# Two latent heads of a pair scored on two row halves of TensorE, with one shared block of rotated keys

## What is computed

```python
def mla_q(zcq, g, w_uq, tabs):
    q = (rms_norm(zcq, g) @ w_uq).reshape(B, L, MLA_HEADS, MLA_NOPE + MLA_ROPE)
    q_nope, q_pe = jnp.split(q, [MLA_NOPE], axis=-1)
    if tabs is not None:
        q_pe = axial_rope(q_pe, tabs)
    return jnp.concatenate([q_nope, q_pe], axis=-1)
...
    k_pe = zkr.reshape(B, L, 1, MLA_ROPE)
    if tabs is not None:
        k_pe = axial_rope(k_pe, tabs)
    k = jnp.concatenate([k_nope, jnp.broadcast_to(k_pe, (B, L, MLA_HEADS, MLA_ROPE))], axis=-1)
...
o_m = block_attention(ql_m, [context keys, latent keys], values, MLA_SCALE)   # softmax(q k^T) v
```

## Time and profile before

| | us |
|---|---|
| Median of 3 runs (945.21 to 947.04) | 945.35 |
| Time of the profiled execution | 945.68 |
| Its span, first to last instruction | 943.8 |
| PE busy | 905.8 (96%) |
| DVE busy | 557.8 (59%) |
| POOL busy | 512.2 (54%) |
| ACT busy | 430.0 (46%) |

### The profile page before, as it was taken

How to read it: one execution, slowest core, us unless ns; L and a number is a source line. 1 busy time by engine, 2 the same in 40 slices (tenths; PEclk the granted TensorE clock), 3 DMA queues, 4 the chain that set the end, 5 groups by cost and what they waited for, 6 DMA issues and landing times.

```text
span 943.8 us, 13413 instructions
## 1 busy us (share of the span) xinstructions
PE 905.8 (96%) x4645; PEld 641.5 (68%) x4645; DVE 557.8 (59%) x903; ACT 430.0 (46%) x879; POOL 512.2 (54%) x433
## 2 busy tenths in 40 slices
PE   5999999999999999999999899999999999999996
PEld 4777767889744565665678789888894445555584
DVE  6669043513578679963218838667246758983337
ACT  6332121414566466655334862235335646655432
POOL 3346223324577755565547437454438886666672
PEclk9999999999999999999999999999999999999999
DMA  9968671214624200020353212223243221020252
GB/s 320 294 224 272 209 248 61 81 38 103 141 52 101 52 18 18 18 68 1 139 167 119 105 32 63 88 83 84 75 115 90 67 52 26 18 76 1 98 170 89
DMA packets 51913, 96.13 MB, mean 102 GB/s; under 512 B 9540, under 2 KB 24752, under 8 KB 50824
## 3 DMA queue, kind: packets, MB, share of 16 engines
q1 hardware_dynamic: 51848, 95.29, 33.3%
HBM read 71.61 MB, written 4.21 MB: 80 GB/s over the span
## 4 chain that ended last, share of the span: by engine, by line
PE 80%; DVE 10%; ACT 4%; POOL 2%; issue 2%; DMA 1%; SPq 1%; POOLq 0%; ACTq 0%; DVEq 0%
PE banks L1003 14%; PE banks L1005 13%; PE banks L1004 13%; PE banks L1306 12%; PE banks L1328 10%; PE banks L1251 4%; DVE negmax L2275 2%; PE banks L1014 2%; PE banks L1347 2%; PE banks L1280 1%; PE banks L1340 1%; DMA w_raw<-in_w_in_dram 1%; DVE area_b L2452 1%; PE banks L1147 1%; PE banks L1468 1%
## 5 line engine op out<-in xcount | busy, mean ns | idle before, releaser
L1989 POOL TENSOR_TENSOR w_split<-w_raw,w_split 128x512 fp32r<-128x512 f32 (+4 forms) x122 | 149.3, 1231 | 214.5 <-ACT w_split L1598 212.8
L1003 PE MATMUL banks<-w_split,area_a 128*128 128x512 f32 (+3 forms) x612 | 232.5, 380 | 4.4 <-DVE area_a L2493 2.1
L1005 PE MATMUL banks<-w_split,area_a 128*128 128x512 f32 (+3 forms) x612 | 224.4, 367 | 0.0
L1004 PE MATMUL banks<-w_split,area_a 128*128 128x512 f32 (+3 forms) x612 | 224.0, 366 | 0.0
L2275 DVE TENSOR_REDUCE negmax<-banks 128x1 f32<-128x768 f32 x160 | 148.1, 950 | 76.7 <-PE banks L1251 55.2
L1598 ACT ACTIVATE w_split<-w_raw 128x512 fp32r<-128x512 f32 (+4 forms) x122 | 69.1, 582 | 195.3 <-PE banks L1005 184.6
L1716 ACT ACTIVATE area_z<-banks 128x512 f32<-128x512 f32 x196 | 108.3, 599 | 74.8 <-PE banks L1306 71.6
L1003 PEld LDWEIGHTS banks<-w_split,area_a 128*128 128x128 f32 x612 | 115.5, 189 | 37.5 <-issue 18.7
L1306 PE MATMUL banks<-area_a 97*128 97x512 f32 (+4 forms) x448 | 127.6, 400 | 4.1 <-ACT area_z L1716 3.0
L1005 PEld LDWEIGHTS banks<-w_split,area_a 128*128 128x128 f32 x612 | 115.3, 188 | 16.7
L1004 PEld LDWEIGHTS banks<-w_split,area_a 128*128 128x128 f32 x612 | 115.8, 189 | 12.9
(11 more groups left out here) (240 smaller groups left out, 1445.2 us busy)
## 6 DMA issues: line engine op xcount, KB each, us to landing
w_raw<-in_w_in_dram SPq DMA_DIRECT2D x32, 512.0 KB, 3.7
area_g<-in_w_ada_dram SPq DMA_DIRECT2D x13, 1024.0 KB, 5.7
area_g<-in_w_ada_dram SPq DMA_DIRECT2D x16, 512.0 KB, 4.8
w_raw<-in_w_out_dram SPq DMA_DIRECT2D x16, 512.0 KB, 4.3
area_a<-parts SPq DMA_DIRECT2D x72, 96.0 KB, 2.2
area_a<-parts SPq DMA_DIRECT2D x30, 192.0 KB, 3.6
area_b<-in_x_dram SPq DMA_DIRECT2D x8, 512.0 KB, 7.1
w_raw<-in_w_in_dram SPq DMA_DIRECT2D x8, 352.0 KB, 5.3
```

Source lines behind the costliest of these rows:

```text
L1003: nc.tensor.matmul(dst, a[0], b[0], start=first, stop=False)
L1004: nc.tensor.matmul(dst, a[0], b[1], start=False, stop=False)
L1005: return nc.tensor.matmul(dst, a[1], b[0], start=False, stop=last)
L1989: op = nc.gpsimd.tensor_tensor(lo, raw, hi.bitcast(F32), ALU.subtract)
```

## The change

- **Operands** (`operands`). A latent pair now has six blocks for both heads: the plain query and plain key, high and low, with head u on rows 64u to 64u+63, and the rotated query of both heads, high and low, with 64 rows per head. Of these 64 rows, 32 hold the rotated query's high part and 32 the same again, so that one pass against a key block holding high and low parts gives two products.
- **Rotated keys** stand once per layer for all latent pairs, in `cmp_t` 6 (high, low, high, low) and 7 (high and a row of ones for the maximum, on both halves), placed by six DMAs (`load_keyrope`) in the place of the per-unit DMAs.
- **Scores**: `latent_passes` lists five passes of 64, 64, 64, 64 and 33 rows; each is issued for head 0 on rows 0 to 63 and head 1 on rows 64 to 127, in alternation, into two ring banks. Both banks must be free before the first pass.
- **Maxima** (`latent_max`): a tile is now one block of 128 queries by 384 keys for both heads: two passes of 64 rows for each of the two heads, each head into its own bank. Eight tiles as before. DVE reduces each tile to two columns of `negpart`, and one more small operation at the end of a pair joins them.
- **Preparation**: the rotated queries of both heads are projected first (`"r"`), then the plain queries (`"q"`) and keys (`"k"`): as many matmuls as before. `rope_high`, `nope_high`, `rope_low`, `nope_low` and one `mla_rope` per pair take the place of the operations per head.
- **Order**: pairs 7 and 8 have an order of their own, `latent_pair`, and `last_pair` is reordered; the ring's list follows. In `latent_pair` the values of the pair before come between scores 0 and 1, and `turn_denominators` and `turn_output` come directly after scores 2 (before: after scores 3 and a maximum tile).

The diff, cut to its core:

```diff
-        PASSES = {"gqa": [(2, 0, 128), (3, 1, 65)], "diff": [(2, 0, 97)], "mla": [(2, 0, 97), (2, 1, 96), (3, 0, 96)]}
+        PASSES = {"gqa": [(2, 0, 128), (3, 1, 65)], "diff": [(2, 0, 97)]}
...
+        def latent_passes(p):
+            q_hi, q_lo, k_hi, k_lo, r_hi, r_lo = operands(2 * p)
+            return [(k_hi, q_hi, 64), (cmp_t[:, 6, :], r_hi, 64), (k_hi, q_lo, 64), (k_lo, q_hi, 64), (cmp_t[:, 7, :], r_lo, 33)]
...
+            def latent_max(L, p, i):
...
+                pe.wait_ge(krope_in, 96 * (L + 1))
+                pe.wait_ge(mla_hi, N_MLA[L, p, "n"])
+                pe.wait_ge(max_read, MAX_BEFORE[m])
...
+                for t, keys, at in todo:
+                    for n, (kf, qf, _) in enumerate(latent_passes(p)[0:2]):
+                        for u in range(2):
+                            r = slice(64 * u, 64 * u + 64)
+                            mm = nc.tensor.matmul(banks[:, b0 + u, at:at + keys.stop - keys.start],
+                                                  qf[r, t * P:(t + 1) * P], kf[r, keys], start=(n == 0), stop=(n == 1))
...
+                if pair_family(p) == "mla":
+                    pe.wait_ge(mla_lo, N_MLA[L, p, "n"])
+                    dsts = [ring_slot("s", L, p, step, u) for u in range(2)]
+                    for kt, cols, at in todo:
+                        passes = latent_passes(p)
+                        for i, (kf, qf, rows) in enumerate(passes):
+                            for u in range(2):
+                                r = slice(64 * u, 64 * u + rows)
+                                mm = nc.tensor.matmul(dsts[u][:, at:at + cols.stop - cols.start], kf[r, kt * P:(kt + 1) * P],
+                                                      qf[r, cols], start=(i == 0), stop=(i == len(passes) - 1))
...
+            def latent_pair(L, p):
+                scores(L, p, 0)
+                max_tile(L, p + 1, 6)
+                values_left(L, p - 1)
+                max_tile(L, p + 1, 7)
+                scores(L, p, 1)
+                max_tile(L, p + 1, 8)
+                denominators(L, p - 1)
+                scores(L, p, 2)
+                turn_denominators(L, p - 1)
+                turn_output(L, p - 1)
+                turn_max(L, p + 1)
...
+            def rope_high(L, p):
...
+                copy(operands(2 * p)[4][:, qcols(L)], qk_t[:, turned_block(L, p), qcols(L)]).then_inc(mla_hi, 1)
+            def nope_high(L, p):
...
+                copy(f[0][:, qcols(L)], qk_t[:, 1, qcols(L)])
+                copy(f[2], qk_t[:, 2, :]).then_inc(mla_hi, 1)
...
-                nc.vector.tensor_tensor(scr[64:96, 0, :], q[96:128], rt[96:128, :], ALU.mult)
-                chain(nc.vector.tensor_tensor(q[64:96], q[64:96], rt[64:96, :], ALU.mult))
-                nc.vector.tensor_tensor(q[64:96], q[64:96], scr[64:96, 0, :], ALU.add).then_inc(mla_roped, 1)
+                chain(nc.vector.tensor_tensor(q, q, rt[:], ALU.mult))
+                for r in range(0, P, 64):
+                    nc.vector.tensor_copy(other[r:r + 32], q[r + 32:r + 64])
+                    op = nc.vector.tensor_copy(other[r + 32:r + 64], q[r:r + 32])
+                chain(op)
+                nc.vector.tensor_tensor(q, q, other, ALU.add).then_inc(mla_roped, 1)
```

More of the change, by code:

```diff
@@ L371 @@
         now, last = _p < NPAIR, _p > 0
+        latent = now and pair_family(_p) == "mla"
         if now:
-            RING += [("s", _L, _p, s, u) for s in range(2) for u in range(2)]
+            RING += [("s", _L, _p, s, u) for s in range(1 if latent else 2) for u in range(2)]
         if last and ctx:
@@ L376 @@
         if now:
-            RING += [("s", _L, _p, 2, u) for u in range(2)]
+            RING += [("s", _L, _p, 1 if latent else 2, u) for u in range(2)]
         if last:
@@ L380 @@
         if now:
[L381 removed]
+            RING += [("s", _L, _p, 2 if latent else 3, u) for u in range(2)]
         if last:
```

320 lines of the change are left out of this document (205 added, 115 removed).

## The result

| | before | changed |
|---|---|---|
| Median of 4 runs each, us | 946.19 (945.21 to 947.06) | 952.10 (951.40 to 952.39) |
| Profiled execution: time, span | 945.68, 943.8 | 952.04, 950.2 |

The ratio is 1.006, with a 95% interval of 1.0048 to 1.0072: the changed kernel is slower by 4.5 to 6.8 us, 5.9 between the medians. The forecast was 3.7 us slower.

What follows compares the result with a forecast made beforehand. TensorE's own stream was taken to bound the kernel, with other engines now and then late around pairs 5 and 6. -9.0 + 12.5 - 4.0 + 4.2 = +3.7 us gave 949.0 us, range 943.0 to 953.5.

Steps and rivals of the forecast that it cites:

- Changes, +12.5: TensorE in both layers: 65 more changes of array division, 57 at about 0.20 us and 8 into values at 0.14.
- Halves: Matmuls on two row halves run side by side; each change to full rows or halves costs about 0.20 us.
- Passes, -9.0: Latent scores on TensorE: 36 steps one pass of 0.23 us shorter, -8.3, and first-layer context steps -0.7 us.
- Ring, +4.2: Latent pairs: new waits for score banks and ScalarE, 1.2 us in pair 7, 0.6 in 8, 0.3 in 9, twice.
- Idle time, -4.0: Six stretches around pairs 4 to 7, both layers: their 7.4 us of PE idle absorbs changes; bounds -1 and -7.4.
- idle down to about half: Sign expected in the profile if right: PE's idle in the stretches of pairs 5 and 6 falls to about half.
- Reductions in the latent pairs, put at nothing: Latent pairs: TensorE's own stream sets them; no cost in the sum for waits on DVE's reductions of maxima tiles.
- The clock: Attention stretches: granted clock is 1.00 in every one, so it was given no part in the forecast.
- 39 changes: Of the 65 added changes of array division, those placed in the stretches with 7.4 us of idle, worth 7.8 us.
- the ring's rival: ACT's bursts hold every latent step, 36 steps of 0.15 to 0.2 us on top: about 954 us; chance 0.14.
- the faster one: DVE and ACT set the stretches around pairs 5 and 6, so changes there cost nothing: about 942 us; chance 0.19.

Runs made afterwards that it cites:

- visit_half: Kernel before plus one 64-row, 128-column matmul ahead of each head's passes in the latent score steps, 72 in all: 973.53 us, ratio 1.0299.
- heads_apart: Changed kernel with each latent score step's ten matmuls issued five for one head, then five for the other, instead of alternating: 960.86 us, ratio 1.0157.
- before_five: Kernel before with the third pass of each pair's second head left out of the latent score steps, five passes instead of six: 942.42 us, ratio 0.9965.
- tiles_together: Changed kernel with latent maxima tiles 0 and 1, and 2 and 3, issued next to each other in pairs 5 and 6: 955.27 us, ratio 1.0096.
- old_order: Changed kernel, halves kept, with pairs 7, 8 and 9 put back into the order of before: 954.14 us, ratio 1.0091.
- rope_last: Changed kernel with VectorE's rotation of the latent queries moved behind the reductions of maxima tiles 4 and 5: 958.48 us, ratio 1.0137.
- values_first: Changed kernel with the first value step (two in pair 7) moved ahead of turning denominators and output, pairs 7 to 9: 950.42 us, ratio 1.0049.

## Why the prediction was right, step by step

The sign and the mechanism held, and so did the prices of a pass and of a change and the size of the ring's term. The number of changes was too high, the term of the idle time too favourable, and two costs were missing.

- **Changes, +12.5.** Right in price, wrong in number. The first layer has 35 changes more, as predicted. The second has 23 more and not 30, so 58 in all and not 65: its `turn_denominators` (L1358) transposes 64 rows and already stood on halves in the kernel before:

```profile
816.52 0.46 PE L1358 MATMUL banks<-ident,scr 64*128 64x64 f32 x4
```

  A change into it was paid there then (the two passes of the tile ahead take 0.52 us to its start in place of 0.36), and a tile of maxima on halves just ahead of it brings no change more. With 50 changes at 0.20 and 8 into the values at 0.14 the term is 11.1 us. The traces, less passes, waits and clock, leave about 6.4 us for the 35 and 4.6 for the 23, 0.18 and 0.20 each; visit_half gives 0.20.
- **Halves.** Between the two halves nothing is paid, in alternation or not. By the Trainium skill (TensorEngine Tiling (Array Packing), section Key Properties) a change of the tile within one mode does not drain the engine; the trace agrees, with starts 0.12 us apart across halves in heads_apart and 0.20 us of gap only where the division changes.
- **Passes, -9.0.** Right on TensorE's stream: the passes of the first layer come to 4.6 to 4.8 us less, those of the second to 4.1, and a step measures 1.15 + 0.2. But the term was treated as if it could be had alone. before_five shows that in the old kernel it is worth 3.3 us, since DVE stands close behind (and by 1.2 us perhaps for the DMA wait told above). In the changed kernel it is worth 7 to 8 of 9, probably because the change also makes DVE lighter; no run tests that by itself. Neither was in the text.
- **Ring, +4.2.** Waits of 1.07, 0.38 and 0.38 us ahead of the output's transposes in the first layer and 0.67, 0.54 and 0.54 in the second, pairs 7, 8 and 9: 3.6, less 0.3 for the one that the kernel before had in pair 9. Predicted 2.4 + 1.2 + 0.6, so pair 7 was put too high and pair 9 too low. Two waits of a score for a bank (0.28 us of idle, 0.35 from start to start, at 840.69 and 860.95 in the second layer) come on top, so the ring took 4.0. The cause was named right: ScalarE copies, rounds and only then frees the bank. The row of pair 7 in the changed kernel:

```profile
401.06 1.57 ACT L1713 ACTIVATE area_a<-area_b 128x768 fp32r<-128x768 f32 x2
...
402.54 1.07 ACT L1835 ACTIVATE late_bias<-banks 128x512 f32<-128x512 f32 x2
...
403.26 0.41 PE L1412 MATMUL banks<-ident,o_t 128*128 128x128 f32 x2 [0.88 <-ACT late_bias L1835]
```

- **Idle time, -4.0.** This step failed in size, and its sign in the profile ("idle down to about half") did not show. The idle of the six stretches went from 7.4 to 7.9 us. Taken from start to start, waits other than the ring's fell by 2.8 us in these stretches, not 4.0. Where ScalarE had held PE in pair 5 of the first layer the wait did shrink, since its rounding copy is shorter. But in pair 6 of the second layer the waits for DVE got longer (0.97 and 0.19 us of idle, where the kernel before has 0.33 and 0.42), at the one place that the prediction had named as longer (3.5 instead of 2.6 us; it is 4.1) and then left inside the sum of the idle.
- **Reductions in the latent pairs, put at nothing.** The prediction let PE wait for ScalarE there, but not for DVE. The two waits for the reduction of a tile (0.68 and 0.52 us of idle, some 1.5 from start to start) are new. before_five says the same of the old kernel: when PE gets early in a latent pair, DVE is next.
- **The clock.** "The granted clock is 1.00 in every stretch, so it has no part in this": true of the attention in the trace of before, wrong for the change. The drop behind this longer wait costs some 1.7 us; what brings it about stays open.

-9.0 + 11.1 + 4.0 - 2.8 + 1.5 + 1.7 = 6.5, against 6.9 in the attention of the two profiled executions. 0.4 us stay without an owner, and the rest of the program is 0.5 shorter, which makes the 6.4 between the spans and 5.9 between the medians. Some luck is in how near the forecast came: 1.4 us of changes that are not there stood in for part of the 4.4 us that the idle time, the reductions and the clock cost more than was forecast.

Two smaller slips of the prediction change nothing in this: 39 changes were placed in the six stretches, and it is 34; and the ring's rival sums to about 955, not 954.

Of the rivals, the faster one assumed that DVE and ScalarE set the stretches of pairs 5 and 6 and that 39 changes would vanish in their waits; tiles_together shows that a tile ahead of a wait can be free. The ring's rival named a real limit: in the old order it does decide (old_order), and the new order is what keeps it small.

## What to carry to other kernels

Count changes of the array's division before counting passes: here one costs about as much as the pass that the halves save, so halves pay only in long runs and not for lone tiles or where full-row work alternates with them. Count from the shapes in the trace: a transpose of 64 rows stands on halves already. Before a saved pass is booked, look for the engine that is just behind TensorE, even where PE's idle is zero: taking one pass out of the old kernel shows it at once. A dependent piece of several microseconds between two deadlines was not helped by moving it, which moved the wait; here it would have to be shorter, or split, which no run tried with everything computed.

## What the runs showed of the hardware that I had not expected

- Matmuls on different row halves overlap although five of one half stand before five of the other in the queue: 1.72 us per step, against 1.36 in alternation.
- A stall of 1 to 2 us on TensorE can be followed by 3.4 us at half the clock (in the changed kernel 1.9 us after the stall's end, in the kernel before at its end), two stalls of rope_last close together by 6.8. It need not be: the stall of 2.1 us in the projections has a drop behind it in nine of fourteen traces, the one of 0.93 to 0.97 us behind the rotation in four of seven, and these four are ones that had no drop in the projections. The two profiled executions of the changed kernel and that of values_first have it at the same place, 813.9 to 817.6 us. It also goes with the spread of the times: in one set the kernel before took 944.9 to 945.7 us at mean clocks of 0.996 and 0.997, and 948.2 to 948.4 at 0.991 and 0.992.
- A full-row matmul of 128 columns set between long ones costs 0.11 us, twice its streaming time.
